# A two-block network on one core: where the operands of the 272-column matmuls lie in on-chip memory

## What is computed

```python
def swiglu(x, w_gate, w_up, w_down):
    return (jax.nn.silu(x @ w_gate) * (x @ w_up)) @ w_down

meta_b = jnp.broadcast_to(meta.astype(x.dtype)[None], (B, N_META, D_MODEL))
h = jnp.concatenate([meta_b, x], axis=1)              # 16 + 256 = 272 tokens
for l in range(DEPTH):                                # DEPTH = 2
    h = h + 0.5 * swiglu(rmsnorm(h, ffn1_norm[l]), ffn1_w_gate[l], ffn1_w_up[l], ffn1_w_down[l])
    h = h + hybrid_mixer(rmsnorm(h, mix_norm[l]), w_in[l], ...)   # proj = u @ w_in, and more
    h = h + 0.5 * swiglu(rmsnorm(h, ffn2_norm[l]), ffn2_w_gate[l], ffn2_w_up[l], ffn2_w_down[l])
```

## Time and profile before

| | us |
|---|---|
| median of three runs | 2168.46 |
| the profiled execution | 2169.23 |
| its span, first to last instruction | 2167.4 |
| TensorE busy in it (18144 matmul records) | 2161.2 |
| VectorE busy | 1474.2 |
| ScalarE busy | 1206.7 |

### The profile page before, as it was taken

How to read it: one execution, slowest core, us unless ns; L and a number is a source line. 1 busy time by engine, 2 the same in 40 slices (tenths; PEclk the granted TensorE clock), 3 DMA queues, 4 the chain that set the end, 5 groups by cost and what they waited for, 6 DMA issues and landing times.

```text
span 2167.4 us, 48351 instructions
## 1 busy us (share of the span) xinstructions
PE 2161.2 (100%) x18144; PEld 2142.3 (99%) x18144; DVE 1474.2 (68%) x2249; ACT 1206.7 (56%) x1759; POOL 286.3 (13%) x327
## 2 busy tenths in 40 slices
PE   9999999999999999999999999999999999999999
PEld 9999999999999999999999999999999999999999
DVE  7655998665566579886657657976656656686663
ACT  6444886544444368755555547865455535565552
POOL 0001661100100136220020011010010010102000
PEclk9999999999999999999999999999999999999999
DMA  7555435556455554455656655355656655455664
GB/s 238 179 191 165 158 126 169 172 174 199 156 179 186 182 164 144 148 181 191 207 178 194 203 185 169 125 177 194 211 172 197 211 176 181 156 171 182 192 218 130
DMA packets 100977, 386.57 MB, mean 178 GB/s; under 512 B 11376, under 2 KB 12528, under 8 KB 100880
## 3 DMA queue, kind: packets, MB, share of 16 engines
q1 hardware_dynamic: 100224, 383.89, 54.5%
q0 software_dynamic: 368, 1.26, 0.2%
q10 hardware_dynamic: 288, 0.12, 0.0%
HBM read 384.18 MB, written 1.05 MB: 178 GB/s over the span
## 4 chain that ended last, share of the span: by engine, by line
PE 91%; DVE 6%; ACT 2%; issue 1%; DMA 0%; SPq 0%; ACTq 0%; DVEq 0%
PE bank L444 28%; PE bank L437 28%; PE bank L445 28%; DVE wlo L460 2%; DVE bank L1795 1%; PE bank L1102 1%; PE bank L1104 1%; PE bank L1103 1%; ACT whi L453 1%; PE bank L1149 0%; PE bank L811 0%; DVE proj L1781 0%; PE bank L993 0%; PE bank L995 0%; PE bank L996 0%
## 5 line engine op out<-in xcount | busy, mean ns | idle before, releaser
L437 PE MATMUL bank<-u,whi 128*128 128x256 f32 (+2 forms) x3776 | 1063.2, 282 | 0.9 <-DVE u L513 0.8
L444 PE MATMUL bank<-u,whi 128*128 128x256 f32 (+1 forms) x3776 | 1060.4, 281 | 0.0
L445 PE MATMUL bank<-u,wlo 128*128 128x256 f32 (+1 forms) x3776 | 1059.0, 280 | 0.0
L460 DVE TENSOR_TENSOR wlo<-raw,whi 128x1024 fp32r<-128x1024 f32 (+1 forms) x673 | 887.0, 1320 | 182.9 <-ACT whi L453 182.4
L453 ACT ACTIVATE whi<-raw 128x1024 fp32r<-128x1024 f32 (+1 forms) x673 | 740.3, 1113 | 198.6 <-PE bank L445 179.7
L437 PEld LDWEIGHTS bank<-u,whi 128*128 128x128 f32 x3776 | 710.3, 188 | 2.7 <-DVE u L513 1.0
L444 PEld LDWEIGHTS bank<-u,whi 128*128 128x128 f32 x3776 | 710.2, 188 | 1.0 <-issue 0.2
L445 PEld LDWEIGHTS bank<-u,wlo 128*128 128x128 f32 x3776 | 710.0, 188 | 0.0
L437 PE MATMUL bank<-hid,whi 128*128 128x256 f32 (+1 forms) x1408 | 394.2, 280 | 0.0
L444 PE MATMUL bank<-hid,whi 128*128 128x256 f32 (+1 forms) x1408 | 394.2, 280 | 0.0
L445 PE MATMUL bank<-hid,wlo 128*128 128x256 f32 (+1 forms) x1408 | 394.2, 280 | 0.0
(11 more groups left out here) (306 smaller groups left out, 2210.9 us busy)
## 6 DMA issues: line engine op xcount, KB each, us to landing
raw<-w SPq DMA_DIRECT2D x548, 512.0 KB, 3.4
raw<-w SPq DMA_DIRECT2D x128, 704.0 KB, 4.8
raw<-w SPq DMA_DIRECT2D x8, 256.0 KB, 6.3
h<-xT SPq DMA_DIRECT2D x4, 272.0 KB, 4.9
outT<-h SPq DMA_DIRECT2D x8, 128.0 KB, 4.6
consts<-cst POOLq DMA_DIRECT2D x1, 576.0 KB, 4.3
dist<-cst POOLq DMA_DIRECT2D x1, 192.0 KB, 2.8
rdist<-cst POOLq DMA_DIRECT2D x1, 192.0 KB, 3.3
```

The costliest lines, as they stand in the source:

```text
L437: pe.matmul(out[:, cut:cols], w, x[:, cut:cols], start=first, stop=False, skip_group_check=True)
L444: pe.matmul(out, w_h, x_lo, start=False, stop=False, skip_group_check=True)
L445: return pe.matmul(out, w_l, x_hi, start=False, stop=last, skip_group_check=True)
L460: dve.tensor_tensor(weights(1, n), raw[:, n % RING, 0:COLS[n]].rearrange("p (k c) -> p k c", c=128), weights(0, n), ALU.subtract).then_inc ...
```

## The change

It alters where operands lie, and no instruction. For `u` in stages 0 to 4 the high and the low part of a tile stand side by side: tile k's high part at element 48 + 640k (2560 bytes from tile to tile), its low part 320 elements behind it in stages 0 to 2 and 288 elements behind it in stages 3 and 4. The weights of the 8-tile panels of stages 0 to 3, and of the first 20 panels of each mixer, start at an offset in their slot of 0 to 112 elements, in steps of 16 (64 bytes), that a table names for each ring slot or panel. The table gives, for high and for low weights apart, the wanted distance between the start of the high column tile and the start of the weight tile, modulo 512 bytes in steps of 64. `hid` gets a layout of its own in each of the stages 0, 2 and 3 and is 11,776 bytes longer in each partition; the buffers behind it in the feed-forward's area move by as much. The 11-tile panels stay at offset 0.

```diff
-U_PLACE = {0: (48, 0), 1: (48, 0), 2: (48, 0), 3: (48, 0), 4: (48, 0), 5: (48, 0), 6: (48, 0), 8: (48, 0), 9: (48, 0), 10: (48, 0), 11: (48, 0), 12: (48, 0), 7: (48, 0)}
+U_PLACE = {0: (48, 320), 1: (48, 320), 2: (48, 320), 3: (48, 288), 4: (48, 288), 5: (48, 0), 6: (48, 0), 8: (48, 0), 9: (48, 0), 10: (48, 0), 11: (48, 0), 12: (48, 0), 7: (48, 0)}
...
+FFN_DISTANCES = {0: ((0, 0), (1, 1), (2, 2), (7, 3)), 2: ((5, 1), (5, 5), (6, 2), (3, 7)),
+                 3: ((7, 7), (3, 3), (3, 7), (7, 3))}
+MIX_DISTANCES = [(p, q) for p in (7, 3) for q in (7, 3, 0, 1, 2, 4, 5, 6)] + [(0, 4), (4, 0), (1, 5), (4, 4)]
+HID_TILES = {0: (384, 24, FT * 384), 2: (384, 24 + 64, FT * 384 - 64), 3: (640, 24, 320)}
+
+def place_of(part, n):
+    y = max(i for i in range(len(PHASES)) if BASE[i]["P"] <= n)
+    j = n - BASE[y]["P"]
+    if COLS[n] != K8 or y > LAST_MIX or PHASES[y] == "mix" and j >= 20:
+        return 0
+    want = MIX_DISTANCES[j] if PHASES[y] == "mix" else FFN_DISTANCES[y][j % RING]
+    return 16 * ((U_PLACE[y][0] // 16 - want[part]) % 8)
...
-            hid = sb("hid", [128, 2 * FT * TILE_STEP + 96], f32r, area)
+            hid = sb("hid", [128, 2 * FT * 384 + 224], f32r, area)
...
         def u_at(y, part, k, c0=None, c1=T):
-            step, first = TILE_STEP if y <= LAST_MIX else SEQ, first_col(y)
-            at = (part * KD + k) * step + sum(U_PLACE[y][:part + 1])
+            first = first_col(y)
+            if y <= LAST_MIX:
+                at = 2 * k * TILE_STEP + U_PLACE[y][0] + part * U_PLACE[y][1]
+            else:
+                at = (part * KD + k) * SEQ + sum(U_PLACE[y][:part + 1])
...
         def hid_at(y, part, f):
-            return tile_of(hid, FT, TILE_STEP if y <= LAST_MIX else SEQ, HID_PLACE[y], y, part, f, first_col(y), T)
+            if y <= LAST_MIX:
+                step, place, low = HID_TILES[y]
+                at = place + part * low
+                return hid[:, at:at + step * FT].rearrange("p (k c) -> p k c", c=step)[:, f, 0:T]
+            return tile_of(hid, FT, SEQ, HID_PLACE[y], y, part, f, first_col(y), T)
...
-            at = META if BASE[LAST_MIX]["P"] + 20 <= n < BASE[LAST_MIX]["P"] + IN_PANELS else 0
+            at = META if BASE[LAST_MIX]["P"] + 20 <= n < BASE[LAST_MIX]["P"] + IN_PANELS else place_of(part, n)
```

## The result

| | before | after |
|---|---|---|
| median, us | 2168.72 (7 runs, 2167.70 to 2169.32) | 2175.74 (7 runs, 2175.28 to 2176.91) |
| the profiled execution, its span | 2169.23, 2167.4 | 2175.28, 2173.5 |

The ratio is 1.0034 [1.0025, 1.0043]: 7.0 us slower, 4.0 more than forecast, inside the range, and over the 0.2% bound.

The account below looks back on a forecast made before the run. TensorE was taken as the bound: matmul count times spacing between starts. Terms of +1.5, +0.9, 0 and +0.6 us summed to +3.0 on the 2168.46 median, giving 2171.5 us, range 2158 to 2183.

Parts of the forecast that it names:

- slower: Outcome of a loss beyond 0.2%, 4.3 us, for the whole kernel; chance 0.34.
- same: Outcome within 0.2%, 4.3 us, of the kernel before, covering the two rivals that lie there; chance 0.41.
- larger loss: Rival: some distances meet the weight load one time more, up to 5.7 ns a matmul; +10.6 us, 2179.1; chance 0.34.
- small loss: The forecast itself: stretches off distance 3 cost slightly more than 123.3 ns; +3.0 us, 2171.5; chance 0.27.
- 2688 matmuls, all at 3: hid's 1584, one ring slot of stages 0 and 2, parts of both mixers: distance stays 3 or 7, cost 0.
- 1632 of the form 3, x, 3: Stage 3 and 288 in each mixer: one matmul in three leaves distance 3, +0.9 ns each, +1.5 us.
- 816 at distance 1: Matmuls moved to distance 1, priced from stage 8's end with 256 columns: 124.4 ns, +1.1 each, +0.9 us.
- 384 gates of mixer 4: 256-column matmuls going to distances 3, 5, 3, priced at a third of 4.4 ns; +0.6 us.
- The 960 without a row: Matmuls at distance 2, 0 or mixed, with no near profile row: set to 0 against today's 123.3 ns.
- The bounds: Limits per matmul where no row was near: 120.0 ns below, 129.0 above, -3.3 and +5.7 around 123.3.
- Placement does nothing: Rival: excess over columns is set by columns, weight load and how a stretch was entered; 2168.5 us; chance 0.14.
- Gain: Rival: some distances avoid one meeting of load and stream, 3.3 ns each on up to 3408 matmuls, 11.4 us; chance 0.25.

Follow-up runs that it names:

- the layouts alone: Changed kernel with every weight panel back at offset 0 and the low part 320 elements behind the high one in stages 0 to 4; 2168.92 us.
- the run between the steps: Changed kernel with distances in quarters and eighths of a step at 272 columns, whole steps at 256, and other hid starts; 2212.47 us, read by panel.
- all at distance 1: Changed kernel with its 4128 offset-panel matmuls at distance 1 and the low part 320 elements behind the high one; 2181.06 us.
- the width experiment: Changed kernel, weights back at slot starts, 256-column gate and up products streaming 260 to 384 columns, extras dropped; 2269.32 us, longer by design, read by panel.
- the run on the shifted low part: Changed kernel, low part 1, 2, 3 steps behind the high in stages 0, 2, 3; slots 0 and 1 keep every load at distance 3; 2173.09 us.

## Why the prediction was right or wrong

**Right.** TensorE's spacing is what moved; the longest wait is 1.2 us before and after. Distances count modulo 4, each panel shows its own price, `hid` and the slots at 3 stay at 123.3 to 123.5, stage 3 is even. The sign and the range held. The loss came to rest 4.0 us above the small one and 3.6 below the larger one, and over the 4.3 us bound, so the outcome "slower", at 0.34, came true and not "same". The largest single chance had stood on the larger loss, while the time I gave was the small loss's; the two were one mechanism at two prices, and its price lay between. That the sum came out positive owes something to luck: none of its three terms had its price from a row that showed it, as the terms below say.

**The sum, term by term.**

| term | forecast | measured |
|---|---|---|
| 2688 matmuls, all at 3 | 0 | 0 (123.3 to 123.5 ns; those of mixer 4 at 124.4, +0.1 us) |
| 1632 of the form 3, x, 3 | +0.9 ns, +1.5 us | stage 3's 1056 +1.1 ns, +1.2 us; the mixers' 576 +1.1 to +3.3 ns, +1.1 us |
| 816 at distance 1 | +1.1 ns, +0.9 us | +3.2 ns, +2.6 us |
| 528 at 2, 336 at 0, 96 mixed | 0 | +3.2, +2.1, +1.6 to +2.6 ns; together +2.6 us |
| 384 gates of mixer 4 | +0.6 us | +0.6 us with the attention between them |
| what follows them, and the later stages | 0 | -1.0 us |
| two panels of mixer 1 that ran at 146.0 and 132.4 ns before, and at 137.5 and 127.0 after | 0 | -0.4 us |
| start of the program | 0 | -0.3 us |

The measured column adds up to 6.5 us, the two traces differ by 6.0. About half of the gap is in stage 0, which would have grown by 2.2 us by these prices and grew by 2.0; the start differs by +0.3 us in the kernel with the layouts alone, so its 0.3 here is no effect of the change that I could show.

*Distance 1* is the term that failed by its row. The earlier trace rows were taken for the price of distance 1, but 256 columns at distance 1 also run at 113.3 ns (the run between the steps), and so does that very stretch in after:

```profile
1421.82 0.28 PE L1107 MATMUL bank<-dy_hi,dw_hi 128*128 128x256 f32 x1
...
1429.75 0.28 PE L1108 MATMUL bank<-dy_lo,dw_hi 128*128 128x256 f32 x1
```

7.93 us over the 70 steps that took 8.24 before. It runs at 113.3 in the layouts alone and at 117.8 with all at distance 1, two kernels that place everything in stage 8 alike. What those rows show is the second spacing of 256 columns and no price of a distance. Two kinds of excess had been put into one.

*The 960 without a row* were set to 0 because 123.3 was the nearest row. The bounds, -3.3 and +5.7, held them, and the value taken did not: all measured lie between +1.6 and +3.2. The lower bound rested on 256 columns, and the width experiment took it away, 272 having the least excess of any width tried above 256. Without that end the middle of what was left, 0 to +5.7, would have been +2.9.

*3, x, 3* had the right size for stage 3 by luck. Mixer 1's end, also one load in three off, was its row, +0.9 ns forecast and +1.1 measured; but a stage with the same shift of the low columns costs that with every load at 3 (the run on the shifted low part). The sum had no term for the shift. In mixer 1, where the weights alone make 3, x, 3, the form cost 1.7 to 3.4 ns.

*The gates* came to what was forecast, again by other parts. In after the spacing settles at 117.5 to 118.1 ns in all sixteen panels. In before it settles at 113.3 or 113.4 in twelve of them, and in each of the seven experiments, none of which shifts the low part in stage 4, in nine to twelve. So the price was nearly all of the 4.4 ns and not a third of it. Inside the panels it comes to 1.1 us, of which the time between them gave back half. As 3, 1, 3 without the shift runs at 113.3 ns in stage 9, the shift of the low columns is the likely cause here too; no run shifts mixer 4 alone. The panels that follow, 117.8 ns before, ran at 113.3 and gave 0.7 us back, and the later stages 0.3. The layouts alone show the same 0.7, and 0.1 of the 0.3, with every distance as before, so the new distances did not earn the most of it. The sum had no term for that.

**The rivals.** *Placement does nothing* falls: the weights' offset alone takes the time from 2168.92 to 2181.06. The Trainium skill (TensorE: Matmul & The Clock Gate, "Step-by-step: what each phase is for") gives the streaming operand and the weight load read ports of their own and says that the load takes no read bandwidth from the running matmul. That placement is then free is not borne out here: 3.1 ns hang on where a 128-column load lies against the stream, and 0.6 to 0.9 when the load is 64 or 32 columns. Whether the ports or something behind them make the difference no run here tells. *Gain* falls: no distance, no eighth of a step and no pair tried gave less than 123.3 ns by more than the trace resolves, and its premise fell with the widths. *Larger loss* had the mechanism, some distances costing more than others, and was nearer than the forecast in the 960 (1.1 us, measured 2.6); its 5.7 ns, borrowed from 512 columns, was not reached by any distance, the most being 3.4 at a whole step (126.7) and 4.7 in the one panel at 1.625 (128.0).

**Open.** Which pairing of addresses decides (the shifted low part shows that load against stream is not all of it); what sets the excess that stays with narrow weights; and what, on entry, picks one of the two spacings at 256 columns.

## What to carry to other kernels

When a change moves addresses only, take the spacing from panel starts in the trace and price each placement by itself; do not borrow a price from a stretch of another width, since two widths can differ by more than any placement does. A row that fits a cause should first be shown to vary with that cause: the one stretch at distance 1 was slow for another reason. When a change moves two things, price each by itself: stage 3's loss was booked on the load and belonged to the shift of its low columns. Where a kernel runs at one placement throughout and nothing is known of others, the nearest row bounds a change badly; here every whole step but the present one cost 2.0 to 3.4 ns.

## What was not expected of the hardware

- The spacing of matmuls is not monotone in the columns: 268 take 125.5 ns and 272 take 123.3; 296 take 139.2 and 304 take 138.7. 256 stands alone with 6.7 ns over its columns, 260 have 11.7.
- 16 bytes count: distance 3.125 is at 123.4 ns and 3.375 at 126.7; 2.5 (123.4) and 1.75 (123.6) are as good as 3 or nearly so.
- At 256 columns distances 1 and 3 can both run at 113.3 ns and 0 and 2 take 118 to 120, while at 272 columns 1 is among the worst (126.7). The best placement belongs to a width.
- A stretch of 256 columns has two steady spacings: the end of stage 8 runs at 117.8 ns before and with all at distance 1, and at 113.3 in after and with the layouts alone.
- A shorter load is not a faster stream: at distance 3, 128 weight columns go with 123.4 ns, 64 with 124.4 and 32 with 124.8.
